# Tables, taps, gate tiles and modulation products moved earlier in a two-layer hybrid kernel, and the last down blocks split by halves of the tokens

## The reference

```python
mod_x = (silu_c @ w_mod[l] + b_mod[l])            # 6 x 1024: shift, scale, gate of both halves
hx = rms_norm(x, g_norm1[l]) * (1 + sc1) + sh1    # the same for ctx with c_ctx
a_val, a_gate, s_bg, s_cg, s_x, c_x, c_g = split(hx @ w_in[l])
u  = conv31(a_val * sigmoid(a_gate)) + conf_b     # Conformer part: 31 taps along rows of 64
ya = silu(layer_norm(u))
yb = s_bg * conv3(s_cg * s_x)                     # short gated convolution: 3 taps
xc = conv4(c_x) + lru_conv_b                      # RG-LRU part: 4 taps
# for both directions: two block-diagonal gates on xc
a = exp(8 * sigmoid(xc @ w_a + b_a) * log_sigmoid(lam))
h = scan(a, sqrt(1 - a * a) * sigmoid(xc @ w_x + b_x) * xc)
yc = (h_forward + h_backward) * gelu(c_g)
x  = x + gt1 * (head_rms_norm([ya, yb, yc]) @ w_out[l])
x  = x + gt2 * feed_forward(modulated norm of x)
```

## Time and profile before

| what | value |
|---|---|
| three runs | 1555.26, 1558.04, 1559.27 us |
| median | 1558.04 us |
| profiled execution, time | 1560.56 us |
| profiled execution, span | 1558.8 us |
| mean granted clock of PE | 0.977 |
| busy: PE, DVE, ACT, GpSimd | 1476.8, 838.1, 619.1, 18.2 us |
| HBM | 392.93 MB read, mean 253 GB/s |

### The profile page before, as it was taken

The page is one execution under the profiler, slowest core; times in us unless marked ns, Lnnn a source line. Parts: engine busy times, 40 slices in busy tenths (PEclk is TensorE's granted clock), DMA queues, the critical chain, the costliest instruction groups (busy, mean ns, idle before and its releaser), DMA issues.

```text
span 1558.8 us, 21878 instructions
## 1 busy us (share of the span) xinstructions
PE 1476.8 (95%) x8674; PEld 1041.6 (67%) x8675; DVE 838.1 (54%) x1139; ACT 619.1 (40%) x702; POOL 18.2 (1%) x60
## 2 busy tenths in 40 slices
PE   6999698999999999896989999999999999999996
PEld 4886486788888887883855576565756566555754
DVE  4799944333333333898564554445645555445552
ACT  4426723232122232549253433434443444434442
POOL 2000000000000000000000000000000000000000
PEclk8999999999999999899989999999999999999998
DMA  9734914822543234349069999989999999999992
GB/s 330 228 108 163 350 60 158 216 61 75 135 109 91 74 92 135 109 135 347 6 266 389 341 327 332 342 329 401 385 408 405 404 384 402 408 356 402 384 409 88
DMA packets 214152, 395.47 MB, mean 254 GB/s; under 512 B 12044, under 2 KB 131232, under 8 KB 214048
## 3 DMA queue, kind: packets, MB, share of 16 engines
q1 hardware_dynamic: 213456, 393.80, 70.7%
q10 hardware_dynamic: 592, 0.21, 0.1%
HBM read 392.93 MB, written 1.05 MB: 253 GB/s over the span
## 4 chain that ended last, share of the span: by engine, by line
PE 84%; DVE 6%; ACT 5%; DMA 3%; issue 2%; DVEq 0%; SPq 0%; ACTq 0%
PE bank L772 82%; DMA raw<-in_moe_w 2%; DMA raw<-in_w_mod 1%; PE bank L1301 1%; ACT w_hi L1738 1%; DVE w_lo L2370 1%; DVE tb L1913 1%; ACT la L1617 1%; DVE lr L2222 1%; DVE y L2062 0%; DVE h_lo L1921 0%; ACT lr L1611 0%; PE bank L1246 0%; ACT lm L1659 0%; DVE li L2209 0%
## 5 line engine op out<-in xcount | busy, mean ns | idle before, releaser
L2370 DVE TENSOR_TENSOR w_lo<-raw,w_hi 128x2048 fp32r<-128x2048 f32 x132 | 302.4, 2291 | 266.2 <-ACT w_hi L1738 263.3
L1738 ACT ACTIVATE w_hi<-raw 128x2048 fp32r<-128x2048 f32 x132 | 252.3, 1912 | 406.2 <-PE bank L772 275.4
L772 PE MATMUL bank<-h_hi,w_hi 128*128 128x512 f32 (+1 forms) x768 | 285.7, 372 | 14.1 <-DVE h_lo L1921 12.0
L772 PE MATMUL bank<-h_lo,w_hi 128*128 128x512 f32 (+1 forms) x768 | 282.7, 368 | 0.0
L772 PE MATMUL bank<-h_hi,w_lo 128*128 128x512 f32 (+1 forms) x768 | 282.5, 368 | 0.0
L1464 ACT ACTIVATE w_hi<-raw 128x2048 fp32r<-128x2048 f32 (+1 forms) x64 | 113.7, 1776 | 195.7 <-PE bank L772 192.8
L772 PEld LDWEIGHTS bank<-h_hi,w_hi 128*128 128x128 f32 x768 | 146.7, 191 | 41.1 <-DVE h_lo L1921 13.9
L772 PEld LDWEIGHTS bank<-h_hi,w_lo 128*128 128x128 f32 x768 | 146.7, 191 | 23.8
L772 PEld LDWEIGHTS bank<-h_lo,w_hi 128*128 128x128 f32 x768 | 147.0, 191 | 23.0
L1896 DVE TENSOR_TENSOR w_lo<-raw,w_hi 128x2048 fp32r<-128x2048 f32 (+1 forms) x64 | 135.9, 2123 | 38.6 <-ACT w_hi L1464 38.5
L772 PE MATMUL bank<-w_hi,hc_hi 128*128 128x512 f32 (+1 forms) x384 | 153.6, 400 | 2.9 <-ACT warm L1793 2.9
(11 more groups left out here) (323 smaller groups left out, 1795.7 us busy)
## 6 DMA issues: line engine op xcount, KB each, us to landing
raw<-in_moe_w SPq DMA_DIRECT2D x220, 1024.0 KB, 9.4
raw<-in_w_mod SPq DMA_DIRECT2D x48, 1024.0 KB, 8.6
raw_x<-in_moe_w SPq DMA_DIRECT2D x44, 1024.0 KB, 9.4
raw<-in_ffn_w SPq DMA_DIRECT2D x44, 512.0 KB, 5.4
raw<-in_w_in SPq DMA_DIRECT2D x18, 1024.0 KB, 5.7
raw<-in_ffn_w SPq DMA_DIRECT2D x16, 704.0 KB, 4.8
raw<-in_w_out SPq DMA_DIRECT2D x8, 1024.0 KB, 5.5
x_in<-in_ctx SPq DMA_DIRECT2D x1, 1024.0 KB, 5.0
```

Source lines behind the costliest of these rows:

```text
L772: return nc.tensor.matmul(dst, lhsT, rhs, start=first, stop=last)
L1738: nc.scalar.activation(w_hi[:, j % SPL, :], raw[:, E_SLOT[j], :], ACT.Copy)\
L2370: V.tensor_tensor(w_lo[:, j % SPL, :], raw[:, E_SLOT[j], :], w_hi[:, j % SPL, :].bitcast(F32), ALU.subtract).then_inc(dve_done, dve_n(name ...
```

## The change

1. **Tables.** Their transposes go to bank 4 (`TABLE`) right after the first quarter's columns; DVE evicts them in the first quarter of the norm and makes the decay rates in the second. ACT's exponential for them goes the same way.
2. **Taps.** Tap 0 of one Conformer block, of the short convolution and of the LRU convolution become ACT activations with scale and bias (`conf_tap`, `sconv_tap`, `lru_tap`). `TAPS` is set anew.
3. **Gate tiles.** Tiles 0 and 1 of the first direction are made by PE in the middle of w_in's blocks 7 and 8, and their activations and DVE work stand between those blocks' splits. They have tiles of their own (`lru(d, t)`) and, for tile 1, banks 6 and 7. `a * a` of these goes from ACT to DVE in layer 1. `CONF_AT` and `MEAN_AT` become 3 in layer 0.
4. **Modulation.** The first batch of `MIX_MODS` is computed after w_in's blocks 3 and 2 (one product each), its loads standing in SP's order behind those of the blocks 5 and 6; its rows are copied by DVE after blocks 5 and 6. The first product of the second batch takes the places between gate tiles that the first batch had.
5. **Feed-forward's end.** The last two down blocks are multiplied for the latents first, then for the context (`last_down`), into banks of their own; squares, root, reciprocal and broadcast of layer 1's norm go by halves, the latents' beside the context's products. `second_products` waits only for the latents' norm, half by half; blocks 0 to 3 of the context's norm follow on DVE, and blocks 4 to 7 behind the split of w_in's fourth block.

The diff, cut to its core:

```diff
-NORM_SPLIT = {(0, 2): ORD[("w_out", 0, NWOUT - 1)], (1, 1): ORD[("down", 1, KD - 1)]}
+NORM_SPLIT = {(0, 2): ORD[("w_out", 0, NWOUT - 1)]}
 def mods_after(c):
+    if c[0] == "w_in" and c[2] in WIN_ORDER[2:4]:
+        l, q = MIX_MODS[c[1]][0][WIN_ORDER.index(c[2]) - 2]
+        return [(l, q, kq) for kq in range(MOD_K)]
     if c[0] == "w_in" and c[2] == WIN_ORDER[-1]:
-        return [(l, q, kq) for batch in MIX_MODS[c[1]] for l, q in batch for kq in range(MOD_K)]
+        return [(l, q, kq) for l, q in MIX_MODS[c[1]][1] for kq in range(MOD_K)]
...
-        TAPS = {0: {"half": 2, 1: 8, 4: 13, 3: 11, 2: 13, 5: 4, 7: 11, 8: 0, "gate": 0},
-                1: {"half": 3, 1: 3, 4: 5, 3: 7, 2: 21, 5: 0, 7: 4, 8: 7, "gate": 4}}
+        TAPS = {0: {"half": 2, 1: 11, 4: 13, 3: 16, 2: 16, 5: 4, 7: 0, 8: 0, "gate": 0},
+                1: {"half": 3, 1: 3, 4: 5, 3: 9, 2: 21, 5: 2, 7: 9, 8: 10, "gate": 0}}
-        CONF_AT = {0: 1, 1: 3}
-        MEAN_AT = {0: 1, 1: 4}
+        CONF_AT = {0: 3, 1: 3}
+        MEAN_AT = {0: 3, 1: 4}
...
+            def last_down():
+                two = [("down", 1, d) for d in (KD - 2, KD - 1)]
+                taken = [take(c) for c in two]
+                for s in (1, 0):
+                    for c, (w, banks) in zip(two, taken):
+                        for k in range(KG):
+                            i = split_mm(banks[1 - s][:, tok(s)], (w[0][:, P * k:P * k + P], w[1][:, P * k:P * k + P]),
+                                         (f_hi[:, k, tok(s)], f_lo[:, k, tok(s)]), k == 0, k == KG - 1)
+                            if (s, c[2], k) == (0, KD - 2, 3):
+                                half_square(1, KD - 2)
+                                half_square(1, KD - 1)
+                            if (s, c[2], k) == (0, KD - 2, KG - 2):
+                                half_root(1)
+                        i.then_inc(pe_done, pe_n("mm_x" if s else "mm", ORD[c]))
+                        if (s, c[2]) == (1, KD - 2):
+                            mean_square(1, 1, slice(0, T), [KD - 3])
+            def second_products():
+                for n in range(2):
+                    for k in range(4):
+                        pe.wait_ge(dve_done, at("h_lo", 1, 1, k, 1))
+                        if k == 0:
+                            take(("w_in", 1, WIN_ORDER[n]))
+                        for t in range(2):
+                            product(1, n, t, k)
+                    if n == 0:
+                        for d in (KD - 2, KD - 1):
+                            half_square(0, d)
+                half_root(0)
+                for k in range(4, KD):
+                    pe.wait_ge(dve_done, at("h_lo", 1, 1, k, 1))
+                    for t in range(2):
+                        for n in range(2):
+                            product(1, n, t, k)
```

PE, both layers, after the first two w_in blocks:

```diff
+                for c in WIN_ORDER[2:7]:
+                    if (l, c) == (1, 5):
+                        pe.wait_ge(dve_done, at("h_lo", 1, 1, KD - 1, 0))
                     project(("w_in", l, c), slice(0, T) if c in (5, 6) else ts, None)
+                    if c in WIN_ORDER[3:5]:
+                        if c == WIN_ORDER[3]:
+                            pe.wait_ge(dve_done, at("t", l, 1, KD - 1, *((0,) if l else ())))
+                        modulation(*MIX_MODS[l][0][WIN_ORDER.index(c) - 3])
+                for q, c in enumerate(WIN_ORDER[7:]):
+                    w, banks = take(("w_in", l, c))
+                    for t in range(2):
...
+                        elif q == 0:
+                            pe.wait_ge(dve_done, at("xc", l, 0))
+                            pe.wait_ge(*evacuated(("w_in", l, WIN_ORDER[6])))
+                            gate(0)
+                        else:
+                            pe.wait_ge(dve_done, at("xc", l, 1))
+                            pe.wait_ge(dve_done, at("mod_row", *MIX_MODS[l][0][1]))
+                            gate(1)
```

ACT, layer 1, around the norm, and both layers' w_in blocks:

```diff
+                    for d in (KD - 2, KD - 1):
+                        half_square(1, d)
+                    half_root(1)
+                    for d in range(3):
+                        half_high(1, d)
+                    hi(ORD[("down", 1, KD - 2)] + SPL)
+                    half_square(0, KD - 2)
...
                     if t:
                         hi(s0 + SPL)
+                        if l == 1:
+                            for d in range(4, KD):
+                                half_high(0, d)
                     nc.scalar.activation(tb[:, t, ts], bank[2 * (s0 % 3) + t][:, ts], ACT.Copy)
...
+                    if c == 7:
+                        act.wait_ge(dve_done, at("clp"))
+                        gates(0, 0)
+                    if c == 8:
+                        gates(0, 1)
+                        gelu(7)
                     act.wait_ge(pe_done, at("mm", s))
                     hi(s + SPL)
+                    if c == 8:
+                        gelu(8)
```

DVE, layer 1's norm, and both layers behind the first w_in block:

```diff
+                    half_normed(1, range(4, KD))
+                    half_inverse(0)
+                    low(ORD[("down", 1, KD - 1)] + SPL)
+                    dve.wait_ge(pe_done, at("rs", 1, 1, 0))
+                    half_normed(0, range(4), 3)
...
                 dve.wait_ge(pe_done, at("mm", s0))
                 low(s0 + SPL)
-                if l == 0:
-                    decay_rates()
+                if l == 1:
+                    half_t(0, 4)
+                    half_normed(0, range(4, KD))
                 dve.wait_ge(act_done, at("evac", s1))
                 gated(1)
...
                     if c in (7, 8):
                         conf_taps(budget[c])
+                        gated_input(0, c - 7)
```

More of the change, by code:

```diff
@@ L923, in started @@
                 quarter_columns(0)
+                pe.wait_ge(table_in, 16 * sum(len(parts) for parts, _, _ in TABLES[1:]))
+                for m in range(1, len(TABLES)):
+                    i = tables(m)
+                i.then_inc(pe_done, pe_n("tables"))
                 for k in range(KD - 2):
@@ L1031, in _ @@
                     columns(*m)
-                modulation(*MIX_MODS[l][1][0])
                 head_sums(l, ts, HEAD_SUM[0], (0, 1))
@@ new lines, in gelu @@
+                def gelu(c):
+                    act.wait_ge(dve_done, at("xc", l, 3))
+                    s = ORD[("w_in", l, c)]
+                    for t in range(2):
+                        nc.scalar.activation(cxp[:, 2 * (c - 7) + t, lo[l] // NC:2, 2:2 + 256],
+                                             bank[2 * (s % 3) + t][:, ts].rearrange("p (s w) -> p s w", w=256),
+                                             ACT.Gelu_apprx_tanh)\
+                            .then_inc(act_done, act_n(*(("evac", s) if t else ())))
@@ L1716, in _ @@
                         act.wait_ge(pe_done, at("mm", s))
-                        if s not in LATE_SPLIT:
-                            hi(s + SPL)
+                        hi(s + SPL)
+                squares(1, 1, slice(0, T), ("down", 1), [KD - 3])
             h_high(1, 2, (1,), hT, "h")
@@ L1936, in normed @@
                             low(1)
+                            dve.wait_ge(pe_done, at("tables"))
+                            for m in range(1, len(TABLES)):
+                                to_columns(m).then_inc(dve_done, dve_n(*(("PT",) if m == len(TABLES) - 1 else ())))
+                            halved()
+                        if c4 == 1:
+                            decay_rates()
                     low(2)
@@ new lines, in half_normed @@
+                def half_normed(s, blocks, last=KD - 1):
+                    for d in blocks:
+                        if d == 0:
+                            half_t(s, 0)
+                        if d < last:
+                            half_t(s, d + 1)
+                        half_low(s, d)
+                if l == 1:
+                    for d in (KD - 2, KD - 1):
+                        down_add(1, d, 1)
+                    half_inverse(1)
+                    dve.wait_ge(pe_done, at("rs", 1, 1, 1))
+                    half_normed(1, range(2))
+                    down_add(1, KD - 2, 0)
+                    half_normed(1, range(2, 4))
+                    low(ORD[("down", 1, KD - 2)] + SPL)
+                    down_add(1, KD - 1, 0)
+                    half_normed(1, range(4, KD))
[3 more added lines that the diff above has]
+                    half_normed(0, range(4), 3)
```

334 lines of the change are left out of this document (198 added, 136 removed).

## The result

The changed kernel takes 1579.47 us (median of 4 runs, 1577.77 to 1581.27), the kernel before 1557.94 (4 runs, 1555.26 to 1559.27): ratio 1.0141, 95% interval 1.0122 to 1.0159.

A forecast was written before the change was run, and what follows sets the result against it. The prediction took TensorE (PE), busy 95% of the span, as the bound, but judged each stretch separately. It summed 8.6 - 8.4 + 16.3 = +16.5 us onto the median 1558.04, forecasting 1574.5 us, range 1560 to 1581 (own range 1569 to 1581).

The forecast's parts named there:

- Layer 0, +8.6: Layer 0: moved products and tiles cost 10.9 us, tables save 0.4, 1.9 comes back after the projections: +8.6 us.
- PE without a gap: Layer 0's projections: PE starts products without a gap, so work inserted between them costs its full price, 10.9 us.
- End of the feed-forward, -8.4: From the last two down blocks to layer 1's third w_in block: halves cut 40.4 us to 32.0, so -8.4 us.
- Layer 1's mixer, +16.3: Layer 1: 10.9 us of moved work plus waits of 3.9, 1.2 and 4.2, less 3.9 given back: +16.3 us.
- the 1.2 us one: Layer 1's projections: PE waits 1.2 us for the fourth modulation load, whose ring slot DVE frees late.
- What comes back behind the projections: Layer 1 after its projections: the chain to the second direction's first tile shortens from 22.7 to 18.9 us, giving back 3.9.
- I put nothing in the sum: Layer 1: slow clock after PE's pauses, about 2 us each, got nothing in the sum and 3 us in the range.
- Rival 1 (loads in time): Layer 1: loads and evictions come in time, so it costs only +7.0 us; whole +7.2, 1565.2 us; chance 0.24.
- the ring's order and not the bandwidth: Layer 1's modulation loads: the ring's order holds them back, not bandwidth; the argument against loads in time, no size given.
- Rival 2 (DVE ends the mixer): Layer 1: DVE's full queue covers PE's extra work, so it costs about nothing; whole +0.2, 1558.2 us; chance 0.14.
- Rival 3 (free in layer 0): Layer 0: inserted work is free because DVE was full too, giving -2.3; whole -3.7, 1554.3 us; chance 0.05.
- Rival 4 (the waits pile up): Layer 1: slow clock and late taps before gate tile 0 cost +25; whole +25.2, 1583 us; chance 0.05.

The follow-up runs named there:

- e11: e4 plus layer 0's two modulation products early again, gate tiles late in both layers: 1559.96 us.
- e5: e4 plus early gate tiles 0 and 1 and the later centring in both layers, modulation products still late: 1561.08 us.
- e10: e5 with nine of layer 0's Conformer taps moved behind the LRU's taps on DVE: 1556.89 us.
- e4: Changed kernel with modulation products, gate tiles and centring late again in both layers and layer 1's first eviction before the half norm; halves, tables, taps stay: 1551.35 us.
- e7: e4 with the context half's norm blocks 4 to 7 moved behind the split of w_in's second block: 1551.24 us.
- e9: e1 with layer 1's early modulation products run on data in SBUF, results unused; the real products and loads stand behind the projections: 1568.65 us.
- e1: Changed kernel with layer 1's eviction of w_in's first block put before the context half's norm blocks 4 to 7 on ACT: 1578.02 us.
- e3: Changed kernel with layer 0's modulation products and gate tiles 0 and 1 back behind its projections and its centring early again: 1571.04 us.
- e6: e1 with the context half's norm blocks 4 to 7 moved behind w_in's second split on ACT and DVE: 1577.77 us.

## Why the prediction came out as it did

By the medians the forecast of +16.5 us is 5.0 short of the +21.5 measured. By stages 1 and 2 it is 7.2 short (1.0 and 6.2), of which the scatter of stage 3 hides a part. So that the time lies within the forecast's own range owes something to luck; the path that was forecast is the one that the trace shows, with one cost missing from it.

- **Layer 0, +8.6: right.** 9.6 in stage 1. The missing 1 us is there when the projections end (11.4 instead of 10.5), 0.60 of it the wait for the taps. The reason given, PE without a gap, holds for the products (e11) but was incomplete for the tiles: DVE's queue was nearly as long as PE's, and only the products beside them hid that (e5, e10).
- **End of the feed-forward, -8.4: mechanism right, size nearly.** The third w_in block of layer 1 starts at 647.8 us (658.12 less the wait and a block), 7.4 us sooner than before when stage 1's shift is taken off. But it is worth less in the end, -5.4 in stage 2 of e4: the half norm that now runs beside the projections fills DVE's queue, and DVE then ends layer 1's mixer (e7). The sum treated the two as separate.
- **Layer 1's mixer, +16.3: right in kind, the slow clock left out.** By the changed kernel's own trace it costs +21.5 (the +14.1 of stage 2 with the 7.4 above put back). PE's waits are as forecast in sum, 9.0 us (4.60, 4.11 and 0.28 at gate tile 0) against 9.3, though the 1.2 us one never came. What comes back behind the projections, 3.6, is near the 3.9. The step that was mis-sized is "I put nothing in the sum" for the clock: 4.2 us, all of it on PE's path, of the 5.2 that are missing. The experiments divide the cost differently, since each wait that goes lets the next one grow. By stage 2 of the traces, from e4 up: gate tiles +1.2 (e5; forecast 3.6 - 3.9), products +5.1 (e9; 7.3), loads and the clock behind them +9.1 (e1; 1.2 + 4.2), the late eviction +4.0 (after; 3.9). Together 19.4, with e4's -5.4 the +14.1. That 4.0 and 3.9 agree is chance: the 4.0 is 1.0 us of waiting and the rest mostly slow clock (e1).
- **Rival 1 (loads in time)** is refuted by the changed kernel's own waits and by e9. Its answer in the prediction, the ring's order and not the bandwidth, is half of it: the ring set when the loads began, the bandwidth how far apart they landed. **Rival 2 (DVE ends the mixer)** is wrong for the changed kernel, where DVE idled 6.29 and 6.74 us, and true for e7. **Rival 3 (free in layer 0)** is refuted by e3 and e11. **Rival 4 (the waits pile up)** came halfway: the clock fell, but gate tile 0 waited only 0.28 us, and for an eviction, not for the taps.

What stays open: how the 9.1 us of the loads divide between the ring's order, DVE's order and the bandwidth. e6 shows that the half norm's place made e1's first wait, and it did not part them for the second product. Open too is what the late eviction costs in an ordinary execution, 1.5 us by the medians or 4.0 by the traces.

## What to carry to other kernels

A weight load that shares a ring with others is released by whoever empties the oldest slot; before moving its consumer forward, follow that slot first, and then count the loads that are issued in a row behind it. Here work inserted in a stretch cost what it issued only where its engine was alone in being full: where a second engine is nearly as full, the parts of a change don't add, and taking one away can expose a wait that another had hidden. A wait removed on its own may be worth less than its length because the next stands behind it; test it also with the next one gone.

## What was not expected of the hardware

After pauses of nearly the same length the clock fell at different moments. Behind the 4.60 us pause of the changed kernel the first product was slow already (0.55 us at 658.12). Behind e1's pause of 4.45 us, 16 instructions ran at full speed first (1.08 us at 667.78), and then the window from 668 to 672 us shows a granted clock of 0.59. Behind the three short pauses of 1.10, 1.49 and 1.52 us of the changed kernel it was down as well: 0.50 from 682 to 688 us. Behind e1's three pauses of 4.45, 1.03 and 1.52 us it was 1.00 again in that stretch.
